# Three places for read tiles, later splits of keys and queries, nearer transposes and a moved weight split in a two-block transformer kernel

## The reference

```python
h = rmsnorm(x, norm1_g)
proj = h @ w_in                      # q 512, k 512, v 512, f_logit 8, u 512 columns
log_f = log_sigmoid(f_logit + b_forget)
c = cumsum(log_f)                    # over positions, one row per head
# 8 heads of 64: causal attention whose logits carry the forget sums
logits = (q / 8) @ k.T + c[query] - c[key];  p = softmax(masked logits);  attn = p @ v
# pool: trailing-window means (2, 4, 8, 16) minus identity, then a 128x128 product each
pooled = window_sum / count - u;     pool = (pooled @ w_pool) * pool_scale
x = x + concat(attn, pool) @ w_out
```

## Time and profile before

| what | value |
|---|---|
| median of 3 runs | 1212.24 us (1210.87 to 1213.34) |
| profiled execution, its own time | 1214.31 us |
| its span in the trace | 1212.5 us |
| TensorE busy | 1141.0 us, 94% of the span |
| VectorE busy | 662.7 us, 55% |
| ScalarE busy | 512.3 us, 42% |
| GpSimd busy | 125.3 us, 10% |
| weight splits, VectorE half (L396) | 181 of 1239 ns mean |
| weight splits, ScalarE half (L388) | 181 of 1058 ns mean |

### The profile page before, as it was taken

One profiled execution on the slowest core, in us unless ns is written; L12 is line 12 of the kernel. 1 busy time (PEld: TensorE's weight loads), 2 busy tenths in 40 slices (PEclk: granted clock), 3 DMA queues, 4 the chain that ended last, 5 costly groups with the idle time before them and its releaser, 6 DMA issues.

```text
span 1212.5 us, 15467 instructions
## 1 busy us (share of the span) xinstructions
PE 1141.0 (94%) x5512; PEld 942.3 (78%) x5512; DVE 662.7 (55%) x1132; ACT 512.3 (42%) x875; POOL 125.3 (10%) x143
## 2 busy tenths in 40 slices
PE   6897978979999999999999996799999999999997
PEld 5675756878888888888898885677888888888886
DVE  6787786776544444433368668736444444443332
ACT  6786686454323233222245457734422332332221
POOL 2375663000000000000000002300000000000000
PEclk9999989989999999999999998899999999999999
DMA  6311100412322322223322212003222222222212
GB/s 257 120 52 45 52 28 1 158 52 87 122 87 103 104 88 102 91 102 103 105 96 88 103 36 70 1 19 121 101 90 104 102 88 91 99 105 104 105 52 70
DMA packets 32515, 106.20 MB, mean 88 GB/s; under 512 B 4048, under 2 KB 6736, under 8 KB 32336
## 3 DMA queue, kind: packets, MB, share of 16 engines
q1 hardware_dynamic: 31712, 104.60, 24.9%
q10 hardware_dynamic: 752, 0.92, 0.3%
HBM read 100.78 MB, written 2.10 MB: 85 GB/s over the span
## 4 chain that ended last, share of the span: by engine, by line
PE 81%; DVE 8%; ACT 7%; issue 3%; DMA 0%; ACTq 0%; POOL 0%; SPq 0%; DVEq 0%
PE bank L475 22%; PE bank L477 22%; PE bank L476 22%; PE bank L960 1%; DVE wl L396 1%; PE bank L950 1%; PE bank L1033 1%; PE bank L1034 1%; PE bank L1035 1%; PE bank L911 1%; PE bank L913 1%; PE bank L912 1%; DVE q L1169 1%; ACT wh L388 1%; PE bank L1903 1%
## 5 line engine op out<-in xcount | busy, mean ns | idle before, releaser
L396 DVE TENSOR_TENSOR wl<-raw,wh 128x1024 fp32r<-128x1024 f32 x181 | 224.1, 1239 | 292.0 <-ACT wh L388 291.8
L388 ACT ACTIVATE wh<-raw 128x1024 fp32r<-128x1024 f32 x181 | 191.3, 1058 | 416.7 <-PE bank L477 268.3
L475 PE MATMUL bank<-hh,wh 128*128 128x512 f32 x872 | 345.3, 396 | 10.4 <-DVE hl L1425 8.6
L477 PE MATMUL bank<-hh,wl 128*128 128x512 f32 x872 | 341.5, 392 | 0.0
L476 PE MATMUL bank<-hl,wh 128*128 128x512 f32 x872 | 341.4, 391 | 0.0
L475 PEld LDWEIGHTS bank<-hh,wh 128*128 128x128 f32 x872 | 164.9, 189 | 47.1 <-issue 10.0
L476 PEld LDWEIGHTS bank<-hl,wh 128*128 128x128 f32 x872 | 165.0, 189 | 35.3 <-issue 1.4
L477 PEld LDWEIGHTS bank<-hh,wl 128*128 128x128 f32 x872 | 164.8, 189 | 35.0
L477 PE MATMUL bank<-gh,wl 128*128 128x512 f32 x308 | 121.7, 395 | 0.0
L475 PE MATMUL bank<-gh,wh 128*128 128x512 f32 x308 | 121.7, 395 | 0.0
L476 PE MATMUL bank<-gl,wh 128*128 128x512 f32 x308 | 121.7, 395 | 0.0
(11 more groups left out here) (240 smaller groups left out, 1671.8 us busy)
## 6 DMA issues: line engine op xcount, KB each, us to landing
raw<-weights SPq DMA_DIRECT2D x181, 512.0 KB, 3.2
xres<-x_t SPq DMA_DIRECT2D x8, 512.0 KB, 6.0
sw<-ta SPq DMA_DIRECT2D x36, 64.0 KB, 2.0
out_t<-final SPq DMA_DIRECT2D x6, 256.0 KB, 2.5
rope<-angles SPq DMA_DIRECT2D x1, 1024.0 KB, 10.8
sw<-ta ACTq DMA_DIRECT2D x4, 64.0 KB, 2.8
wp<-pool_weights ACTq DMA_DIRECT2D x1, 256.0 KB, 2.7
out_t<-final ACTq DMA_DIRECT2D x1, 256.0 KB, 2.4
```

What stands on the lines that cost most here:

```text
L388: act.activation(wh[:, j, :, :], raw[:, j, :, :], ACT.Copy).then_inc(high_split, 1)
L396: v.tensor_tensor(wl[:, j, :, :], raw[:, j, :, :], wh[:, j, :, :].bitcast(F32), ALU.subtract)\
L475: pe.matmul(bank[:, :], wh[:, slot, b, :], ah[:, k, :], start=first and n == 0, stop=False)
L477: ins = pe.matmul(bank[:, :], wl[:, slot, b, :], ah[:, k, :], start=False, stop=last and n == len(blocks) - 1)
```

## The change

```diff
+PE_LEAD = [3] * 5 + [2] * (len(IN2) - 1)
+PE_LEAD[11] = 1
...
+        tx = place("tx", [P, S], at=arena + 70 * KB)
...
-                self.lag = {m: 1 if tiles[m][0] == "plain" else 2 for m in range(n)}
+                self.lag = {m: 2 for m in range(n)}
...
+        def tile_in(m):
+            return tx if m % 3 == 2 else ta[:, m % 3, :]
...
+            begun = 4
             for m in range(n + 4):
-                if 1 <= m < n - 3:
-                    f = m + 3
+                for f in range(begun, min(n, m + 1 + PE_LEAD[m])):
                     slot_wait(pe, ph.c0 + f)
                     if f >= 6:
                         pe.wait_ge(bank_read, ph.t0 + f - 5)
                     products(pe, in_bank(ph, f), ...).then_inc(used, 1)
+                    begun = f + 1
...
         def splits_at(ph, m):
             n = len(ph.tiles)
-            return [m + RING + 2] if m + RING + 2 < n else [m + RING] if n <= m + RING < n + RING else []
+            return [m + RING + 2] if m + RING + 2 < n else []
...
-                    if m >= 2 and ph.tiles[m - 2][0] == "pool":
-                        v.wait_ge(ph.worked, ph.worked_order_count(m - 2))
+                    if m >= 3 and ph.tiles[m - 3][0] == "pool":
+                        v.wait_ge(ph.worked, ph.worked_order_count(m - 3))
...
-                    if m >= 2 and ph.tiles[m - 2][0] == "v":
-                        v.wait_ge(ph.aux, aux_count(ph, ("v", m - 2)))
-                    v.tensor_tensor(ta[rows, m % 2, :], in_bank(ph, m)[rows, :], rstd[rows, :], ALU.mult)\
+                    if m >= 3 and ph.tiles[m - 3][0] == "v":
+                        v.wait_ge(ph.aux, aux_count(ph, ("v", m - 3)))
+                    v.tensor_tensor(tile_in(m)[rows, :], in_bank(ph, m)[rows, :], rstd[rows, :], ALU.mult)\
...
 # vec_attention2, behind the maximum of step n and ahead of ptl and of the reciprocal:
+                if n in (1, 3, 5, 7):
+                    vec_split(v, CHUNK0["out2"] + n // 2)
...
 # act_attention2, behind the exponential of step n:
+                if n in (1, 3, 5, 7):
+                    act_split(act, CHUNK0["out2"] + n // 2)
```

More of the change, by code:

```diff
@@ L578, in pe_in @@
                         for b in range(QB):
-                            ins = pe.transpose(bank[:, b * P:(b + 1) * P], ta[:, tile % 2, b * P:(b + 1) * P], ident[:, :])
+                            ins = pe.transpose(bank[:, b * P:(b + 1) * P], tile_in(tile)[:, b * P:(b + 1) * P], ident[:, :])
                         ins.then_inc(ph.aux, 1)
@@ L641, in vec_work @@
                 w = WINDOWS[i]
-                src, step = ta[:, r, :], 1
+                src, step, own = tile_in(m), 1, tile_in(m)
                 dst = [tb, sw]
@@ L654, in vec_work @@
                 links["v"] += 1
-                link(v, "v", v.scalar_tensor_tensor(tb[:, r, w:S], src[:, w:S], 1.0 / w, ta[:, r, w:S], ALU.mult, ALU.subtract))
-                v.tensor_tensor(tb[:, r, 0:w], acc[:, 0:w], ta[:, r, 0:w], ALU.subtract).then_inc(ph.worked, 1)
+                link(v, "v", v.scalar_tensor_tensor(tb[:, r, w:S], src[:, w:S], 1.0 / w, own[:, w:S], ALU.mult, ALU.subtract))
+                v.tensor_tensor(tb[:, r, 0:w], acc[:, 0:w], own[:, 0:w], ALU.subtract).then_inc(ph.worked, 1)
             elif kind == "forget":
                 v.wait_ge(bank_read, ph.t0 + m + 1)
-                z, l, c = ta[0:8, r, :], sw[0:8, r, :], tb[0:8, r, :]
+                z, l, c = tile_in(m)[0:8, :], sw[0:8, r, :], tb[0:8, r, :]
                 link(v, "v", v.tensor_scalar(z, z, col("b_forget", 0, slice(0, 8)), None, ALU.add))
@@ L674, in vec_finish @@
             if kind == "plain":
-                src = ta[:, r, :]
+                src = tile_in(m)
             elif kind == "forget":
```

## The result

| | before | after |
|---|---|---|
| median of 6 runs | 1212.02 us (1210.87 to 1214.20) | 1218.87 us (1215.72 to 1220.91) |
| ratio, 95% interval | 1 | 1.0052 (1.0035 to 1.0070) |
| span of the profiled execution | 1212.5 us | 1218.3 us |
| from the projection's last product to `out2`'s first | 66.45 us | 71.92 us |
| of it: to the first maximum | 12.61 | 5.34 |

The kernel became slower, as forecast (1216.0, range 1211.5 to 1219.0), and by more: +0.52% where +0.3% was expected. The median of 1218.87 us lies only 0.13 us inside the range. The last six rows are distances between named instructions in each trace: from start to start, but the first two from the product's end (727.03 before and 727.33 after) and the last to the end of the span.

What follows compares the result with a forecast made beforehand. The prediction took TensorE to bound the kernel and its projection, and DVE the gap behind it. It summed -7.2 + 10.0 + 1.0 = +3.8 us, giving 1216.0 us by the median, range 1211.5 to 1219.

Steps and rivals of the forecast that it cites:

- TensorE's projection costs nothing more: Second block's projection: TensorE's 64.7 us stay in the new order, with about 4 us of margin at tile 10; cost nothing.
- First maximum 7.2 us earlier: Between the projection's last product and the attention's first maximum: it comes at 732.4 instead of 739.64, 7.2 us gained.
- the walk: Instruction-by-instruction timing: DVE idle before tile 16 at 727.03, then the four splits at 2.3, 6.6, 10.2, 14.9 us.
- six query halves: DVE's finishes of queries 14, 15 and 16 behind its last reading, 0.72 us each, before the first maximum.
- Start-up 10.0 us longer: First maximum to first `ptl`: the moved splits make DVE and ScalarE run in turn, 16.03 us instead of 6.01.
- The rule against splits beside GpSimd: Attention's start: a split and a GpSimd operation reading SBUF exclude each other; the four splits fall beside none, nothing added.
- The clock, 1.0 us: Behind `ptl` 0: after over 5 us idle, TensorE runs 2 us at half speed, costing 1.0 us.
- upper bound of 1.7 us: The most the low clock behind `ptl` 0 was said to cost; the lower bound was 0.
- Taken back in the rhythm: Rival, first head of the attention: 2 us taken back and no clock cost, +0.8, 1213.0; chance 0.23.
- The splits fit: Rival, attention's start: the splits cost only DVE's 1.14 us each, so -2.6, 1209.6; chance 0.13.
- The projection stalls: Rival, projection: DVE reads tile 10 too late and TensorE waits; 2 us of lateness make 1218.0; chance 0.06.
- Other edits: Chunk loads of `out2` 4 to 7 are issued some 8 us later but wanted only near 812; cost nothing.

Runs made afterwards that it cites:

- e7: e1 with TensorE's lead of three everywhere as before, so the transposes stand where they stood; 1209.03 us, 0.9964 of the kernel before.
- e8: The kernel before with TensorE's new order of transposes alone (two places, old lags, splits in steps 13 to 16); 1206.45 us, ratio 0.9942.
- e5: e1 with the queries finished one step after their reading again, everything else two; 1205.84 us, 0.9938 of the kernel before.
- e3: The kernel after with ScalarE's four split halves moved ahead of its first exponential, VectorE's halves left in place; 1207.04 us, 0.9948 of the kernel before.
- e2: The kernel before with only the four splits moved into the attention, its projection unchanged; 1218.55 us, ratio 1.0049.
- e4: The kernel after with 58 extra unread TensorE products put into its waits at the attention's start; 1214.80 us, 1.0015 of the kernel before.
- e6: e5 with the fourth chunk's split moved behind the attention's last maxima (ScalarE step 35, VectorE step 36); 1206.60 us, 0.9934 of the kernel before.
- e1: The kernel after with the four splits back in the projection's steps 13 to 16, leaving the projection's part alone; 1206.77 us, 0.9951 of the kernel before.

## Why the prediction was right, and where it was not

- **TensorE's projection costs nothing more.** Right: 64.70 us busy of 64.70. The transposes of tile 10 began at 704.23 (I had 703.9, and the whole stage lay 0.30 later), and the reading before them at 700.59 (700.1): 3.6 us from start to start.
- **First maximum 7.2 us earlier.** Right: 5.34 us behind the last product, forecast 5.4, before 12.61. DVE stood idle 3.32 us in front of tile 16, as the walk said. But I credited this to the three parts together. e7 and e8 show that it is the order of TensorE's transposes; the third place and the keys' longer lag are worth at most 0.4 us with it (first maximum 5.18 in e5, 5.54 in e8), and the lag of two on queries costs 1.41 us (e5). The prediction did say that the lag puts "six query halves" behind the last reading, but it gave the lag no price of its own.
- **Start-up 10.0 us longer.** Right: 9.88 (15.89 against 6.01; I had 16.03). The splits began 2.30, 6.56, 10.07 and 14.74 us behind the first maximum, where the walk had 2.3, 6.6, 10.2 and 14.9. Each split cost two hand-overs and both halves, as e3 shows by taking the first engine's half out of the turn.
- **The rule against splits beside GpSimd** (Trainium skill, SBUF — State Buffer, "SBUF: two separate sides"). It was given no time. The start-up came out within 0.14 us of a sum without it, and e2's is the same, as there the splits fell beside no GpSimd operation. But "no row of this case shows the two side by side" was wrong. In the kernel before, in the first layer, a split beside a GpSimd operation took 2.38 us, where the median of all 181 is 1.23:

```profile
76.86 2.38 DVE L396 TENSOR_TENSOR wl<-raw,wh 128x1024 fp32r<-128x1024 f32 x1
76.87 1.28 POOL L1287 TENSOR_TENSOR tb<-ta,rope 128x512 f32<-128x512 f32 x1
```

And in e3 it is the GpSimd operation that takes 1.65 us in place of 0.69. Both agree with the rule.

- **The clock, 1.0 us.** This is the term that was mis-sized. It cost 2.4 to 2.5 us (7.11 against 4.65; e4 takes 2.43 of it away). The idle ahead of it was 4.27 us, where the prediction had over 5. I had ended the window of the earlier trace rows at 742.10 by my own choice and read its length, 2.01 us, as the length of the low clock. The matmuls behind it were as slow: by the windows shown above the clock was low until 744.15, 4.06 us. In the kernel after it was low for 5.38 us. The upper bound of 1.7 us, which was given no working, was too low also. Nor was the low clock before wholly "covered by DVE": with the same code the start-up is 6.01 us there, at 0.62, and 5.36 in e6 at full clock. With 2.4 in place of 1.0 the sum is +5.2. The profiled spans differ by 5.8: -7.27, +9.88 and +2.46 make +5.07, the rest of the attention (fifth `ptl` to `out2`) adds 0.40, and 0.33 lie ahead of the stage and behind it. The medians differ by 6.85; the last 1.05 us stand in no trace.
- **Rivals.** "Taken back in the rhythm" was wrong: nothing came back from the fifth `ptl` on (43.58 against 43.18), and before it the clock took more. "The splits fit" was wrong for this order of instructions, but e3 makes it true, by letting ScalarE run ahead: 3.43 us under before, where that rival's sum had 2.6. "The projection stalls" did not happen.
- **Other edits.** The later chunk loads cost nothing: the stretch behind the attention is 419.05 against 419.02 us.

## What to carry to other kernels

When a job is made of two halves on two in-order engines that already hand work to each other, moving it into that hand-over costs both halves and both waits, not one half alone; look for a place where the first engine can make its half before the second needs it. A change that reorders the engine that is never idle can be free there and worth much on the others; try it alone before adding buffers. When the clock's price is wanted from a trace, first find the stretch's ends by the pace of the instructions, and then ask the window for its length.

## What the runs showed of the hardware

TensorE's clock stayed at its lower level for 4.06 us behind an idle of 5.78 us and for 5.38 us behind one of 4.27 us, busy all the time in both; with the waits filled (e4) it stayed at 1.00. What that costs depends on the stage: nothing where the other engines set the pace (start-up of the kernel after, 15.89 us, against 15.90 in e4), 1.2 us between two start-ups of the same code without the splits (6.57 us at 0.52 in e1, 5.36 at 1.00 in e6), 2.4 us in the first head (7.11 against 4.68 in e4). The Trainium skill says that the throttled clock is the default and that activity releases it (TensorE: Matmul & The Clock Gate, "What's actually happening"). e4 agrees.

A VectorE operation with two inputs in SBUF and a GpSimd operation that ran beside it went with a longer time of one of the two: 2.38 us in place of 1.23 for the split at 76.86 in the kernel before, 1.65 in place of 0.69 us for the multiplication at 737.41 in e3.

The same code ahead of the change took different times from execution to execution: the projection's last product ended at 727.03 us before, 727.33 after, 724.64 in e1 and 722.14 in e2. In the first 60 us the granted clock was 0.97 in the first two and 1.00 in the last two. That spread of 5 us is as large as the effect. The distances within a trace repeat much better: from the fifth `ptl` to `out2` it is 43.16 to 43.18 us in the eight kernels other than the one after (43.58) and e6. But each kernel has one trace only, and in e3 and e7 it shows less of a gain than the runs do.
